# Layer 1: six heads' query weights read once into the latent attention's weight tiles and kept for both tiles

## The reference

```python
q = (x @ w_q).reshape(B, S, PEER_HEADS, 2, PEER_DK // 2)          # 8 heads, 2 halves of 128
s = jnp.einsum('bshcd,cnd->bshcn', q, sub_keys)                   # 128 keys a half
sv, si = lax.top_k(s, PEER_TOPK)                                  # 16 of 128, twice
cand_s = sv[..., 0, :, None] + sv[..., 1, None, :]                # 256 pairs, the best 16 of them
hid = jax.nn.gelu(jnp.einsum('td,ted->te', xt, u[et]), approximate=False)
y   = jnp.einsum('te,ted->td', gt * hid, v[et])                   # gate: softmax of the 16 scores
```

## Time and profile before

| | |
|---|---|
| median of three runs | 1689.02 us (1688.6 to 1692.29) |
| the profiled execution, its own time | 1690.12 us |
| its span, first to last instruction | 1687.8 us |
| PE busy | 1427.3 us (85%) |
| DVE busy | 1026.1 us (61%) |
| ACT / POOL busy | 480.1 / 482.9 us |
| read from HBM | 613.12 MB, 364 GB/s over the span |
| gathers (q0), share of 16 engines | 536.90 MB, 77.3% |
| loads and stores (q1) | 77.30 MB, 12.1% |

### The profile page before, as it was taken

The page is one execution under the profiler, slowest core; times in us unless marked ns, Lnnn a source line. Parts: engine busy times, 40 slices in busy tenths (PEclk is TensorE's granted clock), DMA queues, the critical chain, the costliest instruction groups (busy, mean ns, idle before and its releaser), DMA issues.

```text
span 1687.8 us, 15896 instructions
## 1 busy us (share of the span) xinstructions
PE 1427.3 (85%) x4970; PEld 746.9 (44%) x4970; DVE 1026.1 (61%) x2772; ACT 480.1 (28%) x1236; POOL 482.9 (29%) x522
## 2 busy tenths in 40 slices
PE   8996699888898889997779979998889887777876
PEld 6775344433353445543335644444334433333322
DVE  1113766767767776677532366666676776666764
ACT  1112333333322332222113333333332222222221
POOL 0000333323333333333400023332333333333331
PEclk9997899999999999999988999999999999999999
DMA  9713999999999999999960389999999999999995
GB/s 338 301 52 90 415 420 418 419 406 406 420 420 406 419 420 418 419 398 415 421 274 1 86 329 421 405 420 418 422 418 408 397 422 420 416 421 418 409 416 234
DMA packets 95859, 615.21 MB, mean 364 GB/s; under 512 B 10784, under 2 KB 11040, under 8 KB 29600
## 3 DMA queue, kind: packets, MB, share of 16 engines
q0 software_dynamic: 73728, 536.90, 77.3%
q1 hardware_dynamic: 22048, 77.30, 12.1%
HBM read 613.12 MB, written 1.05 MB: 364 GB/s over the span
## 4 chain that ended last, share of the span: by engine, by line
PE 37%; DMA 35%; DVE 20%; issue 3%; ACT 3%; DVEq 1%; another core or an unknown queue 1%; SPq 0%; POOLq 0%; ACTq 0%
DMA uv<-in_peer_uv_dram,expert 34%; PE y L452 18%; DVE uv L1165 9%; PE spare L355 4%; PE px L252 4%; PE y L324 3%; PE y L262 2%; ACT diag L880 1%; PE spare L275 1%; DVE key_idx L1073 1%; DVE key_left L1065 1%; DVE key_idx L1067 1%; PE y L315 1%; PE spare L288 1%; PE spare L289 1%
## 5 line engine op out<-in xcount | busy, mean ns | idle before, releaser
L452 PE MATMUL y<-uv,diag 128*128 128x512 f32 x2048 | 978.3, 618 | 179.6 <-ACT diag L880 178.7
L1165 DVE CUSTOM_DVE_ANT_0 uv<-px,uv 128x1024 f32<-128x1024 f32 x512 | 618.9, 1221 | 385.8 <-DMA uv<-in_peer_uv_dram,expert 380.8
L776 POOL DMA_INDIRECT uv<-in_peer_uv_dram,expert x512 | 481.7, 941 | 1177.9 <-PE y L452 879.8
L452 PEld LDWEIGHTS y<-uv,diag 128*128 128x128 f32 x2048 | 376.8, 195 | 672.5 <-issue 374.1
L880 ACT ACTIVATE diag<-ident,wts 128x128 f32<-128x128 f32 x512 | 177.5, 394 | 482.2 <-DVE wts L1171 453.7
L874 ACT ACTIVATE act_hid<-hid 128x2 f32<-128x2 f32 x256 | 52.0, 203 | 485.7 <-DVE hid L1165 481.8
L355 PEld LDWEIGHTS spare<-hT,wb_rows 128*128 128x128 f32 x1024 | 124.4, 195 | 27.0 <-issue 23.4
L355 PE MATMUL spare<-hT,wb_rows 128*128 128x128 f32 x1024 | 127.1, 279 | 3.0 <-DVE hT L1046 3.0
L252 PE MATMUL px<-hT,uv 128*128 128x256 f32 x256 | 62.2, 393 | 8.1 <-DMA uv<-in_na_w_dram 8.1
L874 ACT ACT_TABLE_LOAD x50 | 64.2, 1283 | 0.9
L252 PEld LDWEIGHTS px<-hT,uv 128*128 128x128 f32 x256 | 48.0, 195 | 18.6 <-issue 12.7
(11 more groups left out here) (172 smaller groups left out, 956.4 us busy)
## 6 DMA issues: line engine op xcount, KB each, us to landing
wb_rows<-in_peer_w_q_dram SPq DMA_DIRECT2D x64, 512.0 KB
uv<-in_na_w_dram SPq DMA_DIRECT2D x24, 512.0 KB, 10.5
uv<-in_peer_uv_dram,expert POOLq DMA_INDIRECT x512
bias<-in_na_bias_dram SPq DMA_DIRECT2D x16, 256.0 KB
uv<-in_na_w_out_dram SPq DMA_DIRECT2D x8, 512.0 KB, 5.5
wb_rows<-in_na_w_out_dram SPq DMA_DIRECT2D x8, 512.0 KB
uv<-in_mla_w_out_dram SPq DMA_DIRECT2D x8, 512.0 KB, 9.9
wb_rows<-in_mla_w_out_dram SPq DMA_DIRECT2D x8, 512.0 KB
```

What stands on the lines that cost most here:

```text
L452: last = T.matmul(Y[t][:, c, :], diag[:, n % RING, :], uv[:, n % RING, 1, c * 512:(c + 1) * 512], start=False, stop=(k == TOPK - 1 and g % ...
L776: pool.indirect_dma_start(uv[:, n % RING, :, :].rearrange("p h d -> p (h d)"), None, uv_table, bass.IndirectOffsetOnAxis(ap=expert[:, g, k ...
L1165: V_.tensor_tensor_reduce(out=rows, in0=px[:, :, :], in1=rows, scale=1.0, scalar=0.0, op0=ALU.mult, op1=ALU.add, accum_out=hid[:, k:k + 1] ...
```

## The change

Layer 1 keeps the query weights of heads 0 to 5. Their twelve 512 KB pieces go into the tiles of the latent attention, each after its last read: head 0 into `w_latkv`, 1 into `w_kn`, 2 into `w_vu`, 3 into `w_latq`, 4 into `w_qn`, 5 into `w_qr` and `w_qs`. Both tiles' queries read them there. SP issues these loads between the out-projection loads of the gap and the side loads of layer 1, behind a wait for the last product of each old weight. The kept pieces fall out of the order of the side ring. The rows of the last norm go into `V` instead, after the last out-product of the tile.

```diff
+KEPT = 6
-        last_rows = w_latkv[:, :, :].rearrange("p k n -> p (k n)")
-        g_row, b_row = last_rows[:, 0:D], last_rows[:, D:2 * D]
+        g_row, b_row = V[:, 0, :], V[:, 1, :]
+        kept_in = [w_latkv[:, :, :].rearrange("p k n -> p (k n)"), w_kn[:, :, :, :].rearrange("p r j n -> p (r j n)"),
+                   w_vu[:, :, :].rearrange("p r n -> p (r n)"), w_latq[:, :, :].rearrange("p k n -> p (k n)"),
+                   w_qn[:, :, :, :].rearrange("p r j n -> p (r j n)")]
+        kept = [[w[:, c * D:(c + 1) * D] for c in range(2)] for w in kept_in]
+        kept.append([w[:, :, :, :].rearrange("p r j n -> p (r j n)") for w in (w_qr, w_qs)])
...
+        s_kept = [sem(f"kept_queries_landed{h}") for h in range(KEPT)]
...
+        def is_kept(layer, g):
+            return layer == 1 and g % PH < KEPT
+
         side_no = {}
         for layer in range(LAYERS):
             for g in range(3):
                 for c in range(2):
-                    side_no["q", layer, g, c] = len(side_no)
+                    if not is_kept(layer, g):
+                        side_no["q", layer, g, c] = len(side_no)
...
             def queries(layer, g, c, b):
                 t = g // PH
-                w = side_item("q", layer, g, c).rearrange("p (k n) -> p k n", k=DK)
+                if is_kept(layer, g):
+                    pe.wait_ge(s_kept[g % PH], 32)
+                    w = kept[g % PH][c].rearrange("p (k n) -> p k n", k=DK)
+                else:
+                    w = side_item("q", layer, g, c).rearrange("p (k n) -> p k n", k=DK)
...
             def side_load(src, *name):
+                if name[0] == "q" and is_kept(name[1], name[2]):
+                    return
...
                 if layer:
+                    sp.wait_ge(s_y, 4 * PAIRS)
                     sp.dma_start(g_row, ln_ffn_g[1:2, :].partition_broadcast(P)).then_inc(s_rows, 16)
                     sp.dma_start(b_row, ln_ffn_b[1:2, :].partition_broadcast(P)).then_inc(s_rows, 16)
...
             for j in range(PAIRS):
                 line_load("O", pair_no(1, 0, j), mla_w_out[j])
+            last_read = [(2, ("lat", latent_no(1, 0))), (5, ("upK", 1, 1)), (3, ("upV", 1, 1)), (4, ("lat", latent_no(1, 1))),
+                         (3, ("upQ", 1, 1)), (3, ("qpe", 1, 3))]
+            for h in range(KEPT):
+                sp.wait_ge(s_full[last_read[h][0]], job[last_read[h][1]])
+                for c in range(2):
+                    sp.dma_start(kept[h][c], peer_w_q[1, h, c]).then_inc(s_kept[h], 16)
             layer_loads(1)
```

More of the change, by code:

```diff
@@ L200, in program @@
                 for c in range(2):
-                    side_no["q", layer, g, c] = len(side_no)
+                    if not is_kept(layer, g):
+                        side_no["q", layer, g, c] = len(side_no)
             for j in range(PAIRS):
-                if j + 3 < PH:
+                if j + 3 < PH and not is_kept(layer, j + 3):
                     side_no["q", layer, j + 3, 0] = len(side_no)
                 side_no["O", pair_no(layer, 1, j)] = len(side_no)
-                if j + 3 < PH:
+                if j + 3 < PH and not is_kept(layer, j + 3):
                     side_no["q", layer, j + 3, 1] = len(side_no)
```

## The result

| | before | changed |
|---|---|---|
| median, first comparison | 1690.65 us (1688.6 to 1692.33, 4 runs) | 1674.42 us (1672.72 to 1679.86, 4 runs) |
| ratio | | 0.991 (95%: 0.9883 to 0.9937) |
| second comparison (run 1 below) | 1686.37 us (17 runs) | 1673.25 us (6 runs), 0.9904 (0.9885 to 0.9924) |
| profiled execution, span | 1690.12, 1687.8 | 1679.86, 1678.1 |
| read from HBM | 613.12 MB | 606.82 MB |

The change makes the kernel faster, by 16.2 us in the first comparison and 13.1 in the second. Forecast were 21.5 us, and 1667.5 within 1664 to 1674: the time lies 0.4 us above the range. The sign and the bytes were right, a quarter (first comparison) to two fifths (second) of the gain was missing.

The account below looks back on a forecast made before the run. DMA was taken to bound the second expert phase: eighteen loads at 1.25 us save 22.5, 1 is given back for TensorE, so -21.5 from 1690.12 gives 1668.6, or 1667.5 for the median; range 1664 to 1674.

Parts of the forecast that it names:

- What bounds the kernel: Second expert phase: DMA engines are never out of work, share 1.00 at 412 GB/s, so it lasts as its bytes take.
- Price of a load: Second expert phase: each 512 KB load costs 1.25 us of DMA time, with ends 1.13 to 1.30.
- Part 1: Loads that disappear while DMA is full: 33 before, 15 after, eighteen fewer at 1.25, saving 22.5 us.
- Parts 2, 3 and 4: Loads moved into the hole between phases, loads moved into the ramp, waits added on SP and TensorE: each cost 0.
- rival C: Ramp: loads ahead of the loop delay the first rows by 8.7 us, removed ones were free; slower, 1697.7, chance 0.05.
- part 3: Ramp: seven moved loads fit; VectorE's unexplained wait 4 us shorter would be swallowed by a DMA full until 996.8.
- Part 5: Steps 12 to 60: TensorE's 29.5 to 31.4 us a cycle stays below DMA's 32.5; 1 us given back, bounds 0 to 7.5.
- Rival A: First 60 steps: TensorE takes over, only the second tile's twelve loads pay, 15.0 us; 1674.0, chance 0.12.
- Rival B: Loads ran beside the gathers for nothing, hidden by eight slots in flight; 1689.0, chance 0.03.
- end (c) of the price: Four cycles with twelve loads against 48 steps without: 13.6 us more, 1.13 us a load.

Follow-up runs that it names:

- run 1: The changed kernel again with no edit, timed beside the kernel before: 1673.25 us, ratio 0.9904.
- run 8: The kernel before, with seven of eight products left out of queries of heads 3 to 7, layer 1's first tile: 1690.66 us, 1.0005 to the kernel before.
- run 2: The changed kernel with kept weights serving the first tile only, the second loading its pieces as before: 1687.55 us, 1.0002 to the kernel before.
- 3: The changed kernel with kept weights serving the second tile only, the first loading its pieces as before: 1672.98 us, 0.991 to the kernel before.
- run 12: The changed kernel without the ranking of groups 2 and 3 in layer 1, which reuse group 1's expert numbers: 1665.32 us, 0.987 to the kernel before.
- run 7: The changed kernel, with seven of eight products left out of queries of heads 3 to 7, layer 1's first tile: 1668.43 us, 0.9868 to the kernel before.
- 5: The changed kernel with VectorE's row maxima of the scores in layer 1 at cycle offset 7 instead of 5: 1676.82 us, 0.9918 to the kernel before.
- 6: The changed kernel; layer 1's second half of queries at offset 2 instead of 0, key scores at 4 instead of 3: 1673.48 us, 0.9903 to kernel before.
- 9: The kernel before with nine ring slots instead of eight: 1679.39 us, 0.9952 to the kernel before.
- 10: The changed kernel with kept weights for the second tile only and nine ring slots: 1667.3 us, 0.9872 to the kernel before.
- 11: The changed kernel with nine ring slots, layer 1's second half of queries at offset 2, key scores at 4: 1665.38 us, 0.9875 to the kernel before.

## Why the prediction was off

- **What bounds the kernel: wrong in one stretch.** "The phase lasts as long as its bytes take", read from a DMA share of 1.00, was true of steps 96 to 252 and only half the truth in 12 to 48. There a second limit of the same length lay under the first. The chain of waits said it, had I asked it for this stretch and not for the whole span. Before the change, from 1027.75 to 1128.54:

```profile
by line: PE y L452 36.2%; DMA uv<-in_peer_uv_dram,expert 17.6%; PE spare L355 11.2%; DVE uv L1165 6.9%; PE y L324 5.1%; PE spare L288 3.1%; PE spare L289 3.1%; issue 2.3%; PE spare L315 1.8%; ACT L816 1.3%; ACT L874 1.3%; ACT diag L880 1.2%
```

  Gathers have 18% of this chain. Over 1552 to 1660, late in the same phase, they have 69%. In run 8, with the same loads and less TensorE work, they have 34% of it.
- **Price of a load: right.** 1.25 was taken, 1.18 measured (twelve loads, run 2 against the changed kernel; 1.17 and 1.29 against runs 1 and 3), inside 1.13 to 1.30. The second tile's twelve were forecast at 15.0 and paid 14.2.
- **Part 1, eighteen loads: the count was right** (33 before, 15 after), the multiplication wrong: the six of the first tile paid nothing that runs 2 and 3 can tell, and 7.5 us is far outside their intervals.
- **Parts 2, 3 and 4, moved loads and added waits: right**, cost 0. So rival C has nothing: the first add came 121.6 us after the last of the first phase, as before. One remark of part 3 was wrong, that a full DMA would swallow the 4 us if VectorE's unexplained wait went away. The long wait is gone in runs 1 and 12, with the same moved loads. Between the phases they took 1.8 and 3.8 us less, and run 1's second phase was no longer for it (672.9 us to 672.8).
- **Part 5 is the step that failed**: "TensorE stays below, in bursts that a ring of eight should cover. I give 1 us back". It set TensorE's 29.5 to 31.4 us against 32.5 of DMA. TensorE's figure was fair: without the ranking the cycles take 31.3 to 31.8 with TensorE busy 30.95 of them. DMA's was a little high; by the same sum they would take 32.0 (four loads in three cycles). What it left out is VectorE: over 6 us of work for each ranking (57.0 us busy in run 12 for 69.7 in run 1, two rankings less), whose last part stands before the dots in two of three cycles, the wait of about 2 us that this gives TensorE, and the fall of its clock that may follow. These made 33.3 to 34.8 us of such a cycle, over DMA's 32.5 and about equal to the 34.1 (12 x 2.53 + 3 x 1.25) that DMA needed with three loads. The term was sized 1 us and measures 6: eighteen loads at 1.18 are 21.2, and the phase got 15.2. That is near the upper of the bounds given for it (0 to 7.5).
- **Rival A** gave the right time in the first comparison, 1674.0 for 1674.42, at a chance of 0.12; its gain of 15.0 us lies between the two measured, 16.2 and 13.1. Its mechanism was half right: TensorE was the engine that everyone waited for (run 7), but by VectorE's doing (run 12), not by its plain work. Rival B was true of steps 12 to 48 alone, by runs 2 and 3.
- Its argument against B, 13.6 us for twelve loads, compared stretches with different other work. In the changed kernel steps 12 to 60 have seven loads for twelve, the last 48 still none, and the difference is as large, 13.8 us:

```profile
1033.19:1168.11 134.92, 127.04 (x433) 62.99 (x433) 87.92 (x236) 48.73 (x119) 45.57 (x48) 0.97 0.98 393
1542.50:1663.60 121.10, 95.43 (x230) 40.28 (x229) 77.27 (x196) 27.70 (x81) 41.22 (x44) 0.97 0.97 398
```

  So it can't be read as the price of loads, and end (c) of the price was near the measured one by luck.

The fastest kernel of the study is 4: nine ring slots and the kept weights, 1662.87 us (0.9851).

## What to carry to other kernels

A DMA share of 1.00 says that the DMA is one limit, not that it is the only one; ask the chain of waits for the same stretch, and if the transfers have a fifth of it, suspect that fewer bytes will show little. It is a sign and no measure: the changed kernel's two profiles give the gathers none of that chain and 19% of it. Less work for the other engine, with and without the bytes (runs 7 and 8), is what shows it. Before pricing removed bytes, work out for each stretch what a cycle takes without them, all engines and their periodic work included, and count a removed transfer only down to that floor. Once the bytes are off, the next lever is whatever pauses TensorE: here the ranking, worth 5.7 us. A ninth slot gave 10.4 us, by a way that stays open.

## What the runs showed of the hardware

- A pause of about 2 us at TensorE sometimes cost more than itself. In the changed kernel's first profile the add behind it took 2.96 and 3.41 us (1.88 to 1.98 otherwise), with a granted clock of 0.95 over the cycle, and PE was busy 32.5 us for instructions that took 30.95 in run 1's first cycle, which had the same pause of 2.13 us and kept its clock at 1.00. In the eleven profiles with full queries and full ranking the first two cycles each have such a pause of 1.9 to 2.3 us, and the clock fell in 12 of the 22. What decides it is open.
- The wait of some 4 us ahead of VectorE's first rotation, which the prediction could not explain, follows the comparison and not the kernel. VectorE stands 9.8 to 10.0 us there in some profiles and 5.95 in the others. The changed kernel has the long wait in its first profile (121.6 us between the phases) and not in run 1, which is the same code (119.8). It is there in 5 to 8 (121.4 to 121.7) and not in 2, 3 and 12 (117.7 to 117.9). With nine slots (4, 9, 10, 11) it is short too. The kernel before took 1690.65 and 1690.71 us in the comparisons with the wait, and 1686.37 to 1687.65 in those without. What is waited for stays open; ratios within one comparison are free of it.
